# Loading two panels of each expert one expert ahead, and a cheaper extra pass, in a three-layer float32 kernel

## The reference

```python
def moe(h, router_w, router_b, w_up, b_up, w_down, b_down):
    logits = xt @ router_w + router_b                 # 256 tokens x 32 experts
    top_vals, top_idx = lax.top_k(logits, 4)
    gates = softmax(top_vals)
    ...                                               # tokens sorted by expert
    def expert_block(args):                           # one expert's tokens
        hcat = xblk @ w_up[e] + b_up[e]               # 1024 -> 2048
        x_glu = min(hcat[:, 0::2], 7.0)
        x_lin = clip(hcat[:, 1::2], -7.0, 7.0)
        act = x_glu * sigmoid(1.702 * x_glu) * (x_lin + 1.0)
        return act @ w_down[e] + b_down[e]            # 1024 -> 1024
    ...                                               # gated, summed per token
h = layer_norm(ALPHA * h + moe(h), ln2_g, ln2_b)
```

## Time and profile before

| | us |
|---|---|
| median of 3 runs | 1821.06 |
| lowest and highest run | 1818.43, 1823.85 |
| profiled execution | 1820.22 |
| span in that execution, first to last instruction | 1819.0 |
| PE busy | 1715.8 (94%) |
| DVE busy | 802.0 (44%) |
| ACT busy | 611.8 (34%) |
| POOL busy | 40.9 (2%) |
| HBM read over the span | 535.31 MB, of them 402.7 MB expert panels |

### The profile page before, as it was taken

The page is one execution under the profiler, slowest core; times in us unless marked ns, Lnnn a source line. Parts: engine busy times, 40 slices in busy tenths (PEclk is TensorE's granted clock), DMA queues, the critical chain, the costliest instruction groups (busy, mean ns, idle before and its releaser), DMA issues.

```text
span 1819.0 us, 24786 instructions
## 1 busy us (share of the span) xinstructions
PE 1715.8 (94%) x9490; PEld 1036.3 (57%) x9491; DVE 802.0 (44%) x1137; ACT 611.8 (34%) x795; POOL 40.9 (2%) x77
## 2 busy tenths in 40 slices
PE   8999999999999999999999899999999998999996
PEld 8899997788999898876333233333323232333332
DVE  7854447644444557877222222322222222232234
ACT  6755545554555456553111111211111111121111
POOL 3000001000000300000000000000000000000000
PEclk9999999999999999999999999999999999999998
DMA  9535555312555543357799999999999998999994
GB/s 313 185 140 185 186 189 182 139 47 94 189 190 190 177 145 134 139 166 307 293 427 428 425 426 429 427 429 429 427 429 429 427 428 335 406 429 429 428 429 210
DMA packets 88239, 537.42 MB, mean 295 GB/s; under 512 B 10880, under 2 KB 13032, under 8 KB 63592
## 3 DMA queue, kind: packets, MB, share of 16 engines
q1 hardware_dynamic: 82568, 533.23, 72.8%
q10 hardware_dynamic: 5600, 3.15, 0.6%
HBM read 535.31 MB, written 1.05 MB: 295 GB/s over the span
## 4 chain that ended last, share of the span: by engine, by line
PE 66%; DMA 20%; DVE 8%; issue 3%; ACT 3%; ACTq 1%; PEldq 0%; SPq 0%; DVEq 0%
PE psA L2182 24%; DMA expert_ring<-in_expert_w_up 19%; PE psA L538 13%; PE psB L498 12%; PE psB L521 4%; PE psA L521 2%; PE psB L509 2%; DVE w_low L461 1%; PE psA L2188 1%; PE psB L2211 1%; PE psB L382 1%; PE psA L2173 1%; PE psB L1556 1%; PE psB L2182 1%; ACT activated_T L2478 1%
## 5 line engine op out<-in xcount | busy, mean ns | idle before, releaser
L2182 PE MATMUL psA<-expert_ring,gathered_T 128*64 128x512 f32 x1024 | 456.2, 599 | 27.9 <-DMA expert_ring<-in_expert_w_up 22.9
L2183 PE MATMUL psA<-expert_ring,gathered_T 128*64 128x512 f32 x1024 | 456.2, 599 | 0.0
L461 DVE TENSOR_TENSOR w_low<-panel_ring,w_high 128x1024 fp32r<-128x1024 f32 x244 | 296.2, 1223 | 202.7 <-ACT w_high L454 201.9
L454 ACT ACTIVATE w_high<-panel_ring 128x1024 fp32r<-128x1024 f32 x244 | 254.5, 1055 | 269.2 <-PE psA L538 112.2
L2182 PEld LDWEIGHTS psA<-expert_ring,gathered_T 128*64 128x64 f32 x1024 | 136.3, 138 | 340.1 <-issue 293.1
L2182 PE MATMUL psA<-expert_ring,activated_T 128*64 128x512 f32 x512 | 233.4, 598 | 2.2
L2183 PE MATMUL psA<-expert_ring,activated_T 128*64 128x512 f32 x512 | 233.4, 598 | 0.0
L498 PE MATMUL psB<-hT_high,w_high 128*128 128x256 f32 x712 | 202.3, 284 | 0.0
L498 PE MATMUL psB<-hT_low,w_high 128*128 128x256 f32 x712 | 201.5, 283 | 0.0
L498 PE MATMUL psB<-hT_high,w_low 128*128 128x256 f32 x712 | 201.5, 283 | 0.0
L2682 DVE TENSOR_SCALAR normed<-psA 128x512 f32<-128x512 f32 x32 | 22.1, 692 | 388.9 <-PE psA L2183 388.9
(11 more groups left out here) (469 smaller groups left out, 2466.3 us busy)
## 6 DMA issues: line engine op xcount, KB each, us to landing
expert_ring<-in_expert_w_up SPq DMA_DIRECT2D x128, 2048.0 KB, 23.4
expert_ring<-in_expert_w_down SPq DMA_DIRECT2D x64, 2048.0 KB, 19.4
panel_ring<-in_mlp_w SPq DMA_DIRECT2D x32, 2048.0 KB, 7.9
panel_ring<-in_w_in SPq DMA_DIRECT2D x11, 2048.0 KB, 7.9
panel_ring<-in_fox_w_in SPq DMA_DIRECT2D x6, 2048.0 KB, 8.3
panel_ring<-in_lru_w_in SPq DMA_DIRECT2D x3, 2048.0 KB, 13.3
panel_ring<-in_lru_w_out SPq DMA_DIRECT2D x2, 2048.0 KB, 16.2
panel_ring<-in_fox_w_out SPq DMA_DIRECT2D x2, 2048.0 KB, 7.8
```

Source lines behind the costliest of these rows:

```text
L454: A.activation(part_rows(k.w[n % BUFFERS][0], view), view, ACT.Copy).then_inc(s.w_high, 1)
L461: V.tensor_tensor(w[1], view, w[0].bitcast(F32), ALU.subtract).then_inc(s.w_low, 1)
L2182: M.matmul(ps[0:SLOTS], lhsT, rhs[0], **flags)
L2183: return M.matmul(ps[SLOTS:P], lhsT, rhs[1], **flags)
```

## The change

- `EXPERT_SLOTS` becomes (1, 2, 3, 4, 5, 6) and (1, 2, 7, 0, 5, 6): panels 2 and 3 (`DOUBLE`) have two slots, the other four have one.
- SP's order becomes (e,0), (e,1), (e+1,2), (e+1,3), (e,4), (e,5), until expert 28; expert 29 has its panels 2 and 3 already, and experts 30 and 31 are loaded in plain order. (1,2) and (1,3) are loaded before the MoE in place of (1,0) and (1,1). (e,j) waits for (e-1,j), and for (e-2,j) where j is 2 or 3.
- `extra_down_panel` puts the four quarters of the weight rows side by side, each over 512 output columns, in two halves: 16 products of 512 columns in place of 32 of 256. The sum over the row quarters is made by the scatter product. The result is 1024 wide (`y_x`, `DN_x`), so ACT's and DVE's split runs over 128x1024. The scatter goes to both psB tiles, high part first, then the low part.
- The final sums use psB[0] and psB[1], and the layer norm statistics of token tile 1 are made by ACT (a copy and a square, each with a sum) while DVE works on tile 0.
- Some tiles move (`rw_b`, `xg_x`, `unused`).

```diff
-        self.y, self.y_x = ([sb(n + part, [P, w], F32R) for part in ("_high", "_low")]
-                            for n, w in (("expert_out", 512), ("extra_expert_out", 256)))
+        self.y = [sb("expert_out" + part, [P, 512], F32R) for part in ("_high", "_low")]
+        self.y_x = [sb("extra_expert_out", [P, D], F32R)[:], sb("extra_expert_out_low", [P, D], F32R)[:]]
...
-        self.xrows_x, self.XR_x, self.DN_x = self.xrows[:, 0:256], self.XR[:, 0:256], self.DN[:, 0:256]
+        self.xrows_x, self.XR_x, self.DN_x = self.xrows[:, 0:256], self.XR[:, 0:256], flat(k.psA[:, 2:4, :])
...
-EXPERT_SLOTS = ((1, 2, 3, 4, 5, 6), (7, 0, 3, 4, 5, 6))
+EXPERT_SLOTS = ((1, 2, 3, 4, 5, 6), (1, 2, 7, 0, 5, 6))
+DOUBLE = (2, 3)
...
     def extra_down_panel(odd, j):
         panel = expert_panel(k, odd, 4 + j)
-        for r in range(4):
-            for q in range(4):
-                last = M.matmul(m.DN_x[quarter(q)], m.actT_x[:, j, quarter(r)], panel[:, r, quarter(q, 256)],
-                                start=(j == 0 and r == 0), stop=(j == 1 and r == 3))
+        for half in range(2):
+            for r in range(4):
+                last = M.matmul(k.psA[quarter(r), 2 + half, :], m.actT_x[:, j, quarter(r)], panel[:, r, quarter(half, 512)],
+                                start=(j == 0), stop=(j == 1))
         return last
...
-    def extra_scatter_tile(tt):
-        for part in range(2):
-            for q in range(4):
-                last = M.matmul(m.S_x(q), m.scatter_x[quarter(q), tt * P:(tt + 1) * P], m.y_x[part][quarter(q), :],
-                                start=(part == 0), stop=(part == 1))
+    def extra_scatter_tile(tt, part):
+
+        for half in range(2):
+            last = M.matmul(k.psB[tt][:, half, :], m.scatter_x[:, tt * P:(tt + 1) * P], m.y_x[part][:, quarter(half, 512)],
+                            start=(part == 0), stop=(part == 1))
         return last
...
-            rounds = pair * 2 + odd if j >= 2 else pair
+            rounds = pair if j in DOUBLE else pair * 2 + odd
...
             M.wait_ge(s.summed, 3 + e * 2)
+            M.wait_ge(*act_step(6))
+            M.wait_ge(*dve_step(9))
+            for tt in range(TT):
+                extra_scatter_tile(tt, 0)
             M.wait_ge(*dve_step(10))
-            extra_scatter_tile(0).then_inc(s.extra_pe, 1)
-            M.wait_ge(*dve_step(11))
-            extra_scatter_tile(1).then_inc(s.extra_pe, 1)
+            for tt in range(TT):
+                extra_scatter_tile(tt, 1).then_inc(s.extra_pe, 1)
...
-    for tt in range(TT):
-        M.wait_ge(s.summed, 1 + 2 * NE + tt)
-        scatter_tile(tt).then_inc(s.scattered, 1)
+    M.wait_ge(s.summed, 1 + 2 * NE)
+    scatter_tile(0).then_inc(s.scattered, 1)
...
+    scatter_tile(1, k.psB[1]).then_inc(s.scattered, 1)
...
+    x, unread = m.acc[:, 1, :], flat(k.xn[:])[:, 0:D]
+    A.wait_ge(s.summed, 3 + 2 * NE)
+    A.activation(unread, x, ACT.Copy, accum_out=m.bn[1][:, 1, 0, 0:1]).then_inc(s.ln_root, 1)
+    A.wait_ge(s.ln_var, 4)
+    A.wait_ge(s.ln_root, 4)
+    A.activation(unread, x, ACT.Square, bias=m.mv[1][:, 1, 0:1], accum_out=m.bn[1][:, 1, 0, 1:2]).then_inc(s.ln_root, 1)
...
+    last_sum(0, k.psB[0])
+    V.wait_ge(s.summed, 2 + 2 * NE)
+    variance_dve(k, m, 1, 0, m.acc)
+    last_sum(1, k.psB[1])
+    V.wait_ge(s.ln_var, 3)
+    centre_dve(k, m, 1, 0, m.acc)
...
     def expert_slot_free(e, j):
 
-        n = e * 6 + (j - 5 if j >= 2 else j - 11)
+        n = e * 6 + (j + 1)
         S.wait_ge(s.released, n)
         S.sem_inc(s.settled, 1)
         S.wait_ge(s.consumed, n + COUNTED)
+        S.sem_inc(s.settled, 1)
+
+    def load_expert(e, odd, panels, ahead):
+
+        for j in panels:
+            if j == 4 and ahead:
+                for i in DOUBLE:
+                    expert_slot_free(e - 1, i)
+                    load(e + 1, 1 - odd, i)
+            expert_slot_free(e - (2 if j in DOUBLE else 1), j)
+            load(e, odd, j)
...
-    load(1, 1, 0)
+    load(1, 1, 2)
     S.wait_ge(*slot_free(k, PANELS - 1))
-    load(1, 1, 1)
+    load(1, 1, 3)
     S.wait_ge(*hybrid_done(s, 14))
     for j in range(3, 6):
         load(0, 0, j)
-    for j in range(2, 6):
-        expert_slot_free(1, j)
-        load(1, 1, j)
-    with S.Fori(1, NE // 2) as pair:
+    load_expert(1, 1, (0, 1, 4, 5), True)
+    with S.Fori(1, NE // 2 - 2) as pair:
         for odd in range(2):
-            for j in range(6):
-                expert_slot_free(pair * 2 + odd, j)
-                S.sem_inc(s.settled, 1)
-                load(pair * 2 + odd, odd, j)
+            load_expert(pair * 2 + odd, odd, (0, 1, 4, 5), True)
+    load_expert(NE - 4, 0, (0, 1, 4, 5), True)
+    load_expert(NE - 3, 1, (0, 1, 4, 5), False)
+    for e in (NE - 2, NE - 1):
+        load_expert(e, e % 2, range(6), False)
```

More of the change, by code:

```diff
@@ L1940, in __init__ @@
         self.slot_gate, self.slot_gate_x = (sb(n, [P, 1]) for n in ("gate_of_slot", "extra_gate_of_slot"))
-        self.y, self.y_x = ([sb(n + part, [P, w], F32R) for part in ("_high", "_low")]
-                            for n, w in (("expert_out", 512), ("extra_expert_out", 256)))
+        self.y = [sb("expert_out" + part, [P, 512], F32R) for part in ("_high", "_low")]
+        self.y_x = [sb("extra_expert_out", [P, D], F32R)[:], sb("extra_expert_out_low", [P, D], F32R)[:]]
         self.xrows = sb("gathered_rows", [P, 512])
         self.xg = sb("gathered_T", [P, 4, 2, SLOTS])
-        self.glu, self.lin, self.sig, self.unused = (flat(k.xn[:])[:, 512 * i:512 * i + 512] for i in range(4))
+        self.glu, self.lin, self.sig = (flat(k.xn[:])[:, 512 * i:512 * i + 512] for i in range(3))
+        self.unused = flat(k.xn[:])[:, 1536:1536 + T]
         self.actT = sb("activated_T", [P, 4, P])
@@ L1957, in __init__ @@
         self.ln_cols = sb("ln_columns", [P, 2, KD])
-        self.rw_b = sb("router_w_biased", [P, KD, NE])
+        self.rw_b = self.acc[:, 0, 0:KD * NE].rearrange("p (k n) -> p k n", k=KD)
         self.sums = sb("router_sums", [P, 2, NE])
@@ L1969, in __init__ @@
         self.gated_choice = sb("gated_choices", [P, TT, TOPK, NE])
-        self.xg_x = sb("extra_gathered_T", [P, 2, 4, XSLOTS])
+        self.xg_x = flat(k.xn[:])[:, 1792:2048].rearrange("p (n q s) -> p n q s", n=2, q=4)
         self.bn = [sb("bn_stats", [P, TT, 2, 6]) for _ in range(2)]
@@ L2089, in router_sums_dve @@
     weights = lambda i: m.ln_cols[:, i, :].unsqueeze(2).to_broadcast([P, KD, NE])
-    V.tensor_tensor(m.rw_b[:], m.rw[:], weights(1), ALU.mult).then_inc(*dve.step())
+    V.tensor_tensor(m.rw_b, m.rw[:], weights(1), ALU.mult).then_inc(*dve.step())
     V.tensor_tensor(m.rw[:], m.rw[:], weights(0), ALU.mult).then_inc(*dve.step())
@@ L2205, in down_panel, with scatter_tile @@
         return last
-    def scatter_tile(tt):
+    def scatter_tile(tt, out=m.S):
         for half in range(2):
@@ L2210, in scatter_tile @@
             for part in range(2):
-                last = M.matmul(m.S[:, half, :], m.scatter[r, tt * P:(tt + 1) * P], m.y[part][r, :], start=(part == 0),
+                last = M.matmul(out[:, half, :], m.scatter[r, tt * P:(tt + 1) * P], m.y[part][r, :], start=(part == 0),
                                 stop=(part == 1))
@@ L2432, in moe_pe @@
     M.wait_ge(s.extra_dve, 1 + NE * EXTRAS * EXTRA["dve"])
-    for tt in range(TT):
-        M.wait_ge(s.summed, 1 + 2 * NE + tt)
-        scatter_tile(tt).then_inc(s.scattered, 1)
+    M.wait_ge(s.summed, 1 + 2 * NE)
+    scatter_tile(0).then_inc(s.scattered, 1)
+    M.wait_ge(s.gather_copied, 1 + NE)
+    M.wait_ge(s.gate_summed, 1 + NE)
+    M.wait_ge(s.scatter_made, 1 + NE)
+    scatter_tile(1, k.psB[1]).then_inc(s.scattered, 1)
 def moe_act(k, m):
@@ L2529, in moe_act @@
         second_half(A, s, e, tokens, "act", rest, first_pass, next_pass)
-    for tt in range(TT):
-        deviation_act(k, m, 1, tt)
+    deviation_act(k, m, 1, 0)
+    x, unread = m.acc[:, 1, :], flat(k.xn[:])[:, 0:D]
[4 more added lines that the diff above has]
+    A.activation(unread, x, ACT.Square, bias=m.mv[1][:, 1, 0:1], accum_out=m.bn[1][:, 1, 0, 1:2]).then_inc(s.ln_root, 1)
+    A.wait_ge(s.ln_var, 5)
+    A.activation(m.ln_work[1][:, 1, 1:2], m.ln_work[1][:, 0, 1:2], ACT.Sqrt).then_inc(s.ln_root, 1)
 def moe_dve(k, m):
@@ L2623, in add_tile @@
         return V.tensor_tensor(m.acc[:, tt, :], m.acc[:, tt, :], flat(m.S[:]), ALU.add)
[L2625 to L2629, removed]
     even, odd = (flat(m.U)[:, i::2] for i in range(2))
@@ L2728, in extra_down @@
             low_part(m.y_x, m.slot_gate_x, m.DN_x).then_inc(s.extra_dve, 1)
[L2729 to L2732, removed]
+            for tt in range(TT):
+                V.wait_ge(*extra_step(s, "pe", e, i, 11 + tt))
+                V.tensor_tensor(m.acc[:, tt, :], m.acc[:, tt, :], flat(k.psB[tt][:]), ALU.add).then_inc(s.extra_dve, 1)
         def first_pass():
@@ L2745, in moe_dve, with last_sum @@
     V.wait_ge(s.late, LATE_MOE + 32)
-    for tt in range(TT):
+    def last_sum(tt, out):
```

(19 more changed lines are left out.)

1 line of the change is left out of this document (removed).

## The result

| | before | after |
|---|---|---|
| median, us | 1823.85 (5 runs) | 1808.96 (5 runs) |
| lowest, highest | 1818.43, 1830.49 | 1808.38, 1811.30 |
| profiled execution, us | 1820.22 | 1808.38 |
| span in it | 1819.0 | 1807.2 |
| mean granted TensorE clock | 0.990 | 0.995 |

The ratio is 0.9909, 95% interval 0.988 to 0.9938: 11 to 22 us less, 16.6 at the middle. I had forecast 9.0 less.

The account below looks back on a forecast made before the run. Weight transfers were taken to set the pace, with their halts deciding and PE setting the end after the change; 6.3 + 1.8 + 0.85 = 9.0 us less, from a median of 1821.06 to 1812.0, range 1807.5 to 1816.5.

Parts of the forecast that it names:

- the shorter loop body: PE's expert loop: given no term in the sum, named only as a reason against slower instruction supply.
- the stalls at 1029 and 1049: Rival, PE's instruction supply: 4.50 and 1.79 us, covered before, bare after expert 21; 1818.3 or 1843.5 us, chance 0.08.
- set: PE waits without a releaser, close together; forecast as 6.3 us of stalls, once or in each of five expert pairs.
- Start: First load after the eight early panels: (1,0) issued at about 868.2, landing at 877.0, 6.7 us earlier.
- G: The transfers' gain at the MoE's start: 8.5 us, bounds 6.7 and 9.8.
- Expert 21: The one extra pass: PE keeps 1.8 us, its tail nets 0, transfers save 3 to 5 us.
- PE keeps G less 6.7: At expert 21's last ready panel, PE keeps 8.5 - 6.7 = 1.8 us; the rest goes into ready panels.
- the 0: Tail of expert 21's extra pass: net change 0 for PE, bounds -0.5 and +0.8 us.
- What is late next: After expert 21: transfers end 11.5 to 13.5 us earlier, PE sets the end, 8.1 us earlier.
- The term of 6.3 us: At expert 31: the transfers' bound lay 6.3 us behind PE's, gained once PE sets the end.
- The whole of the order: New order of loads, to the MoE's end: 6.3 + 1.8 = 8.1 us earlier.
- Last norm: Last layer norm: tile 1's statistics leave DVE, 0.85 us less, bounds 0 and 1.7.

Follow-up runs that it names:

- b_copy: The kernel before, unchanged, timed against itself: 1828.6 us, ratio 1.0035.
- order_only: The kernel before with only the new slots and SP's new order of loads: 1826.3 us, ratio 1.0032.
- norm_only: The kernel before with only the new last sums and last layer norm: 1825.0 us, ratio 1.001.
- before_one_pass: The kernel before with expert 21's tokens beyond 64 left out, the unused extra pass code still in the loop: 1816.6 us.
- after_pad: The changed kernel with 160 instructions added in a branch never taken: 1826.0 us, ratio 1.0005.
- before_no_code: The kernel before without expert 21's tokens beyond 64 and without the extra pass code in PE's loop body: 1807.8 us.
- body_norm: The changed kernel with the old slots and old order of loads: 1818.2 us, ratio 0.9961.
- after_copy: The changed kernel, unchanged, run again on another chip: 1811.1 us, ratio 0.9921 to before.
- after_one_pass: The changed kernel with expert 21's tokens beyond 64 left out, so no extra pass runs: 1801.7 us.
- body_only: The kernel before with only the new extra down products, their scatter and what goes with them: 1818.2 us, ratio 0.9964.
- after_hold: The changed kernel with load (1,0) also held until PE is done with (0,2): 1815.7 us, ratio 0.9953.
- after_pad_half: The changed kernel with some 80 instructions added in a branch never taken: 1811.6 us.

## Why the prediction was right or wrong

**The step that failed: the shorter loop body, priced at nothing.** I wrote that the stalls at 1029 and 1049 were covered, that the pace between 1546 and 1709 was flat, and so gave them 0.08 as a danger of the new kernel. They were a cost of the old one. I read where they fell in one execution as where they fall. In six profiles of kernels with the long body (before, b_copy, order_only, norm_only, before_one_pass, after_pad) there are 1, 1, 2, 3, 2 and 3 sets, at 1028 to 1088, at 1202, at 1325, at 1614 to 1639 and at 1742 us; in eight with a shorter body there is none. The shorter body is worth 6.6 us at the median (1824.8 to 1818.2), the spread falls from 27 to 6.7 us, and lengthening the body again with code that never runs costs 14.9 us. The hint was in the numbers that I had: three runs of before spread over 5.4 us, and I took the profiled one for all.

That the stalls are the fetching of PE's instructions can be read in the trace I had, from the queue that I did not look at. In before it moved nine packets from 1028 to 1086 us, and from 1090 to 1800, where no stall of this kind is, the DMA part has no row for it at all:

```profile
q8 instruction: 9, 0.15, 1.2%
```

```profile
q1 hardware_dynamic: 20339, 296.10, 98.4%
```

In all six profiles with the long body each set has nine such packets, spread over the 52 to 58 us from its first stall on. The shorter ones have none behind 918 us, after the first turns of the loop, but for a single packet in before_no_code, with no stall beside it.

**What a set costs.** The prediction priced a set at 6.3 us, the two stalls that it named. The chain of before has a third, and SP's queue shows what all three did to PE:

```profile
1078.57 2.00 issue
```

```profile
1024.38 4.58 SPq L2769 DMA_DIRECT2D expert_ring<-in_expert_w_down  x2
...
1059.66 4.57 SPq L2769 DMA_DIRECT2D expert_ring<-in_expert_w_down  x2
...
1090.14 4.57 SPq L2769 DMA_DIRECT2D expert_ring<-in_expert_w_down  x2
```

The two steps are 35.3 and 30.5 us in place of 27.17: 11.4 us of PE, more than the stalls themselves (8.3). Part of the rest is the clock: behind the first stall PE's granted clock is 0.83 over 1030 to 1040 us (its levels are 1.2 and 2.4 GHz), and the first product takes 1.11 us where the mean is 0.60.

**Start.** Forecast: (1,0) issued 6.7 us earlier, at 868.2 with the MoE's start as before; measured 866.55, with a start 1.6 us earlier, so 6.8 us earlier counted from the start. G was to be 8.5, within 6.7 to 9.8. The 130th panel of the order, (21,3) before and (21,1) after, landed 12.1 us earlier in the first pair of profiles, of which 1.6 lie ahead of the MoE; between body_norm and after_copy it is 6.4, with a start 0.7 earlier. So G is 10.5 in one pair and 5.7 in the other, outside my bounds on either side, with the forecast near the middle. That all of it is made at the start is borne out by after_one_pass.

**Expert 21.** The step "PE keeps G less 6.7" holds in both pairs: 12.1 - 6.7 = 5.4 against 5.2 measured (1486.20 to 1480.99), and 6.4 - 6.7 = -0.3 against -0.4. The extra pass itself: down products 3.64 us (forecast 3.8), ACT 1.11 (1.13), DVE 1.28 (1.3), the low products 1.19 (0.7). From the extra bias products to the next expert's first panel 36.6 us against 36.9, so the 0 was right.

**What is late next.** Right: PE sets the end after expert 21, at 27.16 us per expert, and no wait for a panel appears after 1500 us. The transfers end 14.6 us earlier in the first pair, 13.0 of them behind the MoE's start (forecast 11.5 to 13.5), and this is hidden, as forecast. The term of 6.3 us for it measured 6.4 in the first pair (from the extra bias products to the last sum 317.3 against 310.9 us) and 4.8 in the second. The whole of the order was forecast at 8.1 and measured 7.0.

**Why the order gains nothing with the long body.** In the old order the transfers lie some 6 us behind PE at the end, so a set after expert 21 is partly covered; in the new order PE is bare and the set costs all of it. The profiles show this. The stretch from the extra bias products to the last sum, in us:

| | no set in it | one set in it |
|---|---|---|
| old order | 316.9 to 318.0 (before, body_only, body_norm) | 326.2 (b_copy), 321.9 (norm_only) |
| new order | 310.9 to 312.1 (after, after_copy, after_hold, after_pad_half) | 322.8 (order_only), 322.3 (after_pad) |

The chains of b_copy and of order_only, both with a set at 1742 us:

```profile
1485.10 1.06 PE psA L2244 x8
...
1811.33 1.23 DVE moe_sum L2623
```

```profile
1486.01 1.06 PE psA L2245 x8
...
1808.76 1.23 DVE moe_sum L2624
```

A set costs the new order some 11 us and the old one 4 to 9, so the gain of some 5.7 us shrinks to 3.5 or nothing. With that, order_only and after_pad, which have the new order and the long body, come out at before's time, while body_norm to after_copy gains 7.0.

**Last norm.** DVE from the last sum of tile 0 to its end took 11.6 us against 12.8, better than the forecast 0.85. But the span ends 3.6 us after it against 2.7. The sum of both is 0.3 us, and the times show 0. The forecast left the stores out. That they now come closer together is not the reason: in norm_only they are issued just as close and the span ends 2.7 us after DVE. The stores of norm_only, and then of body_norm (count, size, median us to landing):

```profile
out_x<-moe_sum SPq DMA_DIRECT2D x2, 512.0 KB, 2.6
```

```profile
out_x<-moe_sum SPq DMA_DIRECT2D x2, 512.0 KB, 3.1
```

Why the second store takes longer where the new norm and the new extra pass come together, no run here shows.

**The sum.** Forecast 8.1 + 0.85 + 0 = 9.0. Measured by medians: order 7.0, norm 0, body 6.6, together 13.6 with the two parts taken on two chips, 14.4 by the ratio of after_copy. The first pair of profiles, each with its own stalls, differs by 11.8. The changed kernel's own time was forecast at 1812.0 and came out at 1809.0 and 1811.1; it is the kernel before that was read too fast. Its profiled execution was one whose only set fell early, and its median, 1821.06 over three runs, is 1823.6 to 1825.4 over 18 to 34.

## What to carry to other kernels

Code in a loop that never runs can cost time: where a profile has waits without a releaser in a looped engine, count the instruction packets in several executions, and see whether a shorter body makes them go. When a baseline's own runs spread by more than the effect that is forecast, look for the cause of the spread before anything else, since one profile shows only where it fell this time. And a faster stream of loads is worth only what the engine behind it can hand on after its last long halt.

## What the runs showed of the hardware

By my count of products (two passes and two weight loads for a float32 one) and branches, PE's loop body had 1548 instructions before and 1390 after; with 1474 (after_pad_half) there is no set of stalls, with 1554 (after_pad) there are three. So the limit lies between 1474 and 1548 by this count, which leaves out waits and semaphore steps; the lower side rests on one profile and eight runs. All edits that changed the length of the loop did it in the code that is jumped over, so the length of the body and the length of the jump were not told apart.

Each set goes with nine more instruction packets of 16.4 KB, spread over one turn of the loop (two experts); three profiles have one more behind the loop. Outside the sets the loop runs for stretches of 117 to 831 us with none. The Trainium skill, in "Runtime: NRT & Kernel Launch", section "Instruction fetch mechanics", gives PE a store of 2048 instructions filled in blocks of 256 by its own queue. The packet size agrees with such a block. The figure of 2048 no run here shows. What sets off a new fetch of the body at one time and not at another no run here shows either.
